# Thirteen modulation units added by GpSimd in place of VectorE, in a kernel of two transformer blocks

## The reference

```python
cs = jax.nn.silu(c)
mod = cs @ w_ada[l] + b_ada[l]
sh1, sc1, gt1, sh2, sc2, gt2 = [m[:, None, :] for m in jnp.split(mod, 6, axis=-1)]
h = _rmsnorm(x, g_pre_mix[l]) * (1.0 + sc1) + sh1
```

```python
h = rmsnorm(x, g_pre[i])
o, z = swa_sink_mixer(h, w_in_a[j], sinks_a[j])
y = (o.astype(z.dtype) * jax.nn.silu(z)) @ w_out
x = x + rmsnorm(y, g_post[i])
```

## Time and profile before

| | us |
|---|---|
| three runs | 1829.17, 1830.26, 1831.99 (median 1830.26) |
| the profiled execution | 1828.53 |
| its span in the trace | 1826.2 |
| TensorE busy in the span | 1798.2 (98%) |
| VectorE busy | 1294.4 (71%) |
| ScalarE busy | 895.6 (49%) |
| GpSimd busy | 189.0 (10%) |

### The profile page before, as it was taken

How to read it: one execution, slowest core, us unless ns; L and a number is a source line. 1 busy time by engine, 2 the same in 40 slices (tenths; PEclk the granted TensorE clock), 3 DMA queues, 4 the chain that set the end, 5 groups by cost and what they waited for, 6 DMA issues and landing times.

```text
span 1826.2 us, 25859 instructions
## 1 busy us (share of the span) xinstructions
PE 1798.2 (98%) x8412; PEld 1475.1 (81%) x8412; DVE 1294.4 (71%) x1700; ACT 895.6 (49%) x1265; POOL 189.0 (10%) x268
## 2 busy tenths in 40 slices
PE   8999999999999999999999999999999999999998
PEld 6777768887888888888888888888888888888886
DVE  5888888877977767777678887666666664455445
ACT  6566565455454454544444555444444444444443
POOL 1222221300000000110000130000000000000000
PEclk9999999999999999999999999999999999999999
DMA  8888768556667668698888957777777755555554
GB/s 282 277 270 261 259 215 323 182 171 189 223 217 251 211 215 272 210 321 282 285 281 284 319 186 230 230 230 230 230 230 230 229 191 191 194 195 193 192 191 138
DMA packets 180030, 424.91 MB, mean 233 GB/s; under 512 B 15376, under 2 KB 15616, under 8 KB 179584
## 3 DMA queue, kind: packets, MB, share of 16 engines
q1 hardware_dynamic: 151376, 320.07, 53.3%
q0 software_dynamic: 28304, 103.89, 18.1%
q10 hardware_dynamic: 288, 0.16, 0.1%
HBM read 421.97 MB, written 2.10 MB: 232 GB/s over the span
## 4 chain that ended last, share of the span: by engine, by line
PE 86%; DVE 6%; DMA 3%; ACT 2%; issue 2%; POOL 0%; DVEq 0%; ACTq 0%; POOLq 0%; SPq 0%
PE bank L1771 27%; PE bank L1773 27%; PE bank L1772 27%; DMA ada_raw<-in_w_ada 2%; PE bank L1827 2%; DVE w_lo L1119 2%; DVE acc_a L1129 1%; DMA raw<-in_w_in_a 1%; PE bank L1947 1%; DVE y L1261 1%; PE bank L1927 1%; ACT w_hi L644 1%; ACT y L653 0%; DVE x L1157 0%; PE bank L2066 0%
## 5 line engine op out<-in xcount | busy, mean ns | idle before, releaser
L1119 DVE TENSOR_TENSOR w_lo<-raw,w_hi 128x1024 fp32r<-128x1024 f32 (+1 forms) x608 | 742.4, 1226 | 412.6 <-ACT w_hi L644 411.8
L644 ACT ACTIVATE w_hi<-raw 128x1024 fp32r<-128x1024 f32 (+1 forms) x608 | 635.8, 1050 | 719.6 <-PE bank L1773 671.6
L1771 PE MATMUL bank<-w_hi,h_hi 128*128 128x512 f32 x2272 | 898.9, 396 | 4.3 <-DVE h_lo L1224 1.8
L1773 PE MATMUL bank<-w_hi,h_lo 128*128 128x512 f32 x2272 | 887.2, 391 | 0.0
L1772 PE MATMUL bank<-w_lo,h_hi 128*128 128x512 f32 x2272 | 886.0, 390 | 0.0
L1771 PEld LDWEIGHTS bank<-w_hi,h_hi 128*128 128x128 f32 x2272 | 427.6, 188 | 95.8 <-issue 3.9
L1773 PEld LDWEIGHTS bank<-w_hi,h_lo 128*128 128x128 f32 x2272 | 427.3, 188 | 91.2
L1772 PEld LDWEIGHTS bank<-w_lo,h_hi 128*128 128x128 f32 x2272 | 427.8, 188 | 85.3
L531 POOL DMA_DIRECT2D ada_raw<-in_w_ada x160 | 85.0, 531 | 1009.4 <-DVE acc_a L1129 812.6
L1129 DVE SCALAR_TENSOR_TENSOR acc_a<-ada_raw,cond,acc_a 128x1024 f32<-128x1024 f32 x112 | 143.1, 1278 | 16.1 <-DMA ada_raw<-in_w_ada 15.9
L1129 DVE SCALAR_TENSOR_TENSOR acc_b<-ada_raw,cond,acc_b 128x1024 f32<-128x1024 f32 x48 | 66.0, 1375 | 1.9 <-DMA ada_raw<-in_w_ada 1.9
(11 more groups left out here) (194 smaller groups left out, 1047.0 us busy)
## 6 DMA issues: line engine op xcount, KB each, us to landing
raw<-in_w_ff SPq DMA_DIRECT2D x256, 512.0 KB, 4.3
raw<-in_w_in SPq DMA_DIRECT2D x176, 512.0 KB, 4.5
ada_raw<-in_w_ada POOLq DMA_DIRECT2D x160, 512.0 KB, 5.0
raw<-in_w_in_a SPq DMA_DIRECT2D x72, 512.0 KB, 4.9
ada_more<-in_w_ada POOLq DMA_DIRECT2D x32, 512.0 KB, 5.9
raw<-in_w_out_a SPq DMA_DIRECT2D x32, 512.0 KB, 5.2
raw<-in_w_o SPq DMA_DIRECT2D x32, 512.0 KB, 4.9
raw<-in_w_moba SPq DMA_DIRECT2D x16, 512.0 KB, 4.5
```

The lines of the kernel that those rows point to most:

```text
L644: act.activation(used(w_hi, turn, s), used(raw, turn, s), ACT.Copy).then_inc(hi_ready, 1)
L1119: dve.tensor_tensor(used(w_lo, turn, s), used(raw, turn, s), used(w_hi, turn, s).bitcast(F32), ALU.subtract).then_inc(lo_ready, 1)
L1771: pe.matmul(out_ap, hi, rhs_hi, start=start, stop=False)
L1773: return pe.matmul(out_ap, lo, rhs_hi, start=False, stop=stop)
```

## The change

In each loop iteration GpSimd adds the units u2, u5 and u9 (of u0 to u11), and in the last iteration u0 to u3, all four. It does this with two instructions in place of VectorE's one: the loaded unit is multiplied in place by its number per partition, spread over 1024 columns, and a second instruction, which waits for the first through a new semaphore `ada_scaled`, adds it to the accumulator. `ada_done` becomes two semaphores, one for each half of the columns, because the units of the two halves may now finish out of order.

```diff
+ON_POOL, ON_POOL_LAST = (2, 5, 9), (0, 1, 2, 3)
...
-        ada_done = sem("ada_done")
+        ada_done = [sem("ada_done0"), sem("ada_done1")]
+        ada_scaled = sem("ada_scaled")
...
+            def add_group(i, n, nth):
+
+                part, k = group_k(i, n)
+                pool.wait_ge(ada_loaded[n % 4], (i * 12 + 8 + n - n % 4) * 4 + 16)
+
+                pool.wait_ge(ada_done[n % 2], i * 6 + 4 + n // 2)
+                half = (acc_b if part == SH1 else acc_a)[:, n % 2 * (D // 2):(n % 2 + 1) * (D // 2)]
+                pool.tensor_tensor(ada_slot(n % 4), ada_slot(n % 4),
+                                   cond[:, bass.ds(k + n // 2, 1)].to_broadcast([P, D // 2]), ALU.mult)                    .then_inc(ada_scaled, 1)
+                pool.wait_ge(ada_scaled, i * len(ON_POOL) + nth + 1)
+                pool.tensor_tensor(half, half, ada_slot(n % 4), ALU.add).then_inc(ada_done[n % 2], 1)
...
-            def ada_and_bias(i, units, steps):
+            def ada_and_bias(i, units, adds, steps):
...
                     for j in range(GROUP_A):
                         if steps[j] == n + 1:
                             bias(i, j)
+                    if n - 4 in adds:
+                        add_group(i, n - 4, adds.index(n - 4))
...
                     if s >= 4:
-                        ada_first(i * 12 + 8, s - 4, acc_b, i * 2 + (s - 4) // 2)
+                        if s - 4 not in ON_POOL:
+                            ada_first(i * 6 + 4, s - 4, acc_b, i * 2 + (s - 4) // 2)
...
-                if s >= 4:
-                    ada_first(44, s - 4, acc_b, 6 + (s - 4) // 2)
+                if s >= 4 and s - 4 not in ON_POOL_LAST:
+                    ada_first(22, s - 4, acc_b, 6 + (s - 4) // 2)
```

More of the change, by code:

```diff
@@ L524, in init_acc, with load_ada @@
                 pool.dma_start(acc[0:1, :], b_ada[:, part * D:(part + 1) * D]).then_inc(acc_init[n], 16)
-            def load_ada(m, slot, part, k, half, slots=2, first=False):
+            def load_ada(pairs, n, slot, part, k, slots=2, first=False):
+                half = n % 2
                 if not first:
-                    pool.wait_ge(ada_done, m - slots + 1)
+                    pool.wait_ge(ada_done[half], pairs + n // 2 - slots // 2 + 1)
                 col = part * D + half * (D // 2)
@@ L532, in load_ada, with load_tiles, load_first, group_k @@
                     .then_inc(ada_loaded[slot], 16)
-            def load_tiles(m, part, k, tiles=4):
+            def load_tiles(pairs, part, k, tiles=4):
                 for n in range(2 * tiles):
-                    load_ada(m + n, n % 2, part, k + n // 2, n % 2)
-            def load_first(m, n, part, k):
-                load_ada(m + n, n % 4, part, k + n // 2, n % 2, 4, isinstance(m, int) and m + n < 4)
-            def load_group(i, n):
[L545 to L548, removed]
+                    load_ada(pairs, n, n % 2, part, k + n // 2)
+            def load_first(pairs, n, part, k):
+                load_ada(pairs, n, n % 4, part, k + n // 2, 4, isinstance(pairs, int) and 2 * pairs + n < 4)
+            def group_k(i, n):
+                if n < 4 or n >= 12:
+                    return SH1, i * 2 + (2 - 6 if n >= 12 else 0)
+                return SC1, i * 4 + 2
+            def load_group(i, n):
+                part, k = group_k(i, n)
+                load_first(i * 6 + 4, n, part, k)
+            def add_group(i, n, nth):
+                part, k = group_k(i, n)
+                pool.wait_ge(ada_loaded[n % 4], (i * 12 + 8 + n - n % 4) * 4 + 16)
[5 more added lines that the diff above has]
+                pool.tensor_tensor(half, half, ada_slot(n % 4), ALU.add).then_inc(ada_done[n % 2], 1)
             def bias(i, j):
@@ L590, in _ @@
                 pool.wait_ge(heads_cur, i + 1)
-                ada_and_bias(i, range(12), STEPS)
+                ada_and_bias(i, range(12), ON_POOL, STEPS)
             pool.wait_ge(heads_cur, CHUNKS)
-            ada_and_bias(CHUNKS - 1, range(4 - ADA_AHEAD), STEPS_LAST)
+            ada_and_bias(CHUNKS - 1, range(4 - ADA_AHEAD), ON_POOL_LAST, STEPS_LAST)
             pool.wait_ge(h_lo_ready, H_NORM0 + UPT)
@@ L610, in _ @@
             with pool.Fori(0, 4) as g:
-                load_tiles(g * 8 + 64, GT1, g * 4)
+                load_tiles(g * 4 + 32, GT1, g * 4)
             for n in range(UPT):
-                load_ada(96 + n, n % 2, SH2, n // 2, n % 2)
+                load_ada(48, n, n % 2, SH2, n // 2)
                 if 1 <= n <= 4:
@@ L619, in _ @@
             with pool.Fori(0, CHUNKS - 1) as c:
-                load_tiles(c * 12 + 104, SC2, c * 2, 2)
-                load_tiles(c * 12 + 108, SH2, c * 4 + 4, 4)
-            load_tiles(140, SC2, 6, 10)
+                load_tiles(c * 6 + 52, SC2, c * 2, 2)
+                load_tiles(c * 6 + 54, SH2, c * 4 + 4, 4)
+            load_tiles(70, SC2, 6, 10)
             for j in range(8):
@@ L696, in round_sum @@
             def round_sum(n, part, units):
-                act.wait_ge(ada_done, units)
+                for half in range(2):
+                    act.wait_ge(ada_done[half], units // 2)
                 if n >= 2:
@@ L1120, in split, with add_ada, ada, ada_first @@
                                   ALU.subtract).then_inc(lo_ready, 1)
-            def add_ada(m, slot, acc, k, half, loads):
+            def add_ada(before, slot, acc, k, half, loads):
                 dve.wait_ge(ada_loaded[slot], loads)
-                if not isinstance(m, int) or m > 1:
-                    dve.wait_ge(ada_done, m - 1)
+                if not isinstance(before, int) or before:
+                    dve.wait_ge(ada_done[half], before)
                 part = acc[:, half * (D // 2):(half + 1) * (D // 2)]
                 dve.scalar_tensor_tensor(part, ada_slot(slot), cond[:, bass.ds(k, 1)], part, ALU.mult, ALU.add)\
-                    .then_inc(ada_done, 1)
-            def ada(m, n, acc, k):
-                add_ada(m + n, n % 2, acc, k, n % 2, (m + n - n % 2 - ADA_FIRST // 2) * 8 + 16)
-            def ada_first(m, n, acc, k):
-                add_ada(m + n, n % 4, acc, k, n % 2, (m + n - n % 4) * 4 + 16)
+                    .then_inc(ada_done[half], 1)
+            def ada(pairs, n, acc, k):
+                add_ada(pairs + n // 2, n % 2, acc, k, n % 2, (pairs + n // 2 - ADA_FIRST // 4) * 16 + 16)
+            def ada_first(pairs, n, acc, k):
+                add_ada(pairs + n // 2, n % 4, acc, k, n % 2, (pairs * 2 + n - n % 4) * 4 + 16)
             def y_stats(r, t, squares):
@@ L1410, in _ @@
                         gate_turned(i)
-                    ada_first(i * 12 + 12, s, acc_a, i * 4 + 4 + s // 2)
+                    if s + 4 not in ON_POOL:
+                        ada_first(i * 6 + 6, s, acc_a, i * 4 + 4 + s // 2)
             last = CHUNKS - 1
```

24 lines of the change are left out of this document (12 added, 12 removed).

## The result

| | before | after |
|---|---|---|
| runs on the same chip, median (lowest to highest), us | 1829.72 (1828.02 to 1831.99), 4 runs | 1846.91 (1845.96 to 1848.32), 4 runs |
| the profiled execution, us | 1828.53 | 1847.76 |
| its span, us | 1826.2 | 1846.1 |
| GpSimd busy, us | 189.0 | 260.5 |

The changed kernel is slower: 1.0093 times the time of before, 95% interval 1.0081 to 1.0104, or 17.2 us. The forecast was 1837.8 with a range of 1831 to 1845. The sign was right, the size was not: the time lies above the range.

A forecast was written before the change was run, and what follows sets the result against it. TensorE bounds the loops; only the last iteration, bound by a chain through VectorE, could win. 6.6 there plus 1.0 in the loops is 7.6 us on 1828.53: 1836.1, or 1837.8 as median of runs; range 1831 to 1845.

The forecast's parts named there:

- The prize: Last iteration: at most 3.7 us of TensorE waits and 1.8 of clock can be won, 5.5 in all.
- The price of the new instructions: On GpSimd a product takes 2.2 us and a sum 2.4, so a unit 4.6 (4.4 to 6.4).
- Holding up for whole instructions: VectorE's L1119, L1129, L1250 and L1343 can each be blocked for a whole GpSimd instruction, now 2.2 or 2.4 us.
- rival 1: VectorE keeps the turn where it asks first; h4 and h5 on time, 0.5 to 3.5 us slower, taken as same; chance 0.19.
- Rival 2: No holding up that matters: additions run beside VectorE, last iteration gains 4.4 us, 1825.9; chance 0.09.
- The last iteration: GpSimd and VectorE hold each other up in turn, heads come late, TensorE waits 6.6 us longer for h6.
- The cycle: Last iteration, from one head's neg_cur to the next: 7.3 us, against 5.3 before.
- h6 stays 6.6 late: Last iteration: behind u3 only b7 follows, so h6 keeps h5's lateness of 6.6 us.
- The sign for L1119: Last iteration: VectorE's L1119 (`w_lo`) rows would show above 3 us.
- The loop iterations: Holding mostly covered under a busy TensorE: 0.3 us for each iteration, 1 in all, from bounds of 0 and 1.5 each.
- rival 3: Forecast plus loop stalls of 1.5 to 2 us each, at h7 and h6: 1842 or so; chance 0.12.
- u9 falls into slots with no heads: Loop iterations: u9's product and sum meet no head's work; no price of its own was given.

The follow-up runs named there:

- e6: The kernel before with VectorE's four additions of the last iteration left out and done by nobody: 1824.34 us against 1829.27, -4.9.
- e5: Last iteration only, GpSimd writes zeros about as long in place of product and sum, four additions left out: 1825.72 us against 1829.27 before, -3.6.
- e9: Last-iteration-only kernel with each GpSimd product and sum cut into two instructions of 512 columns: 1832.16 us against 1829.48 before, +2.7.
- e2: GpSimd adds only u0 to u3 of the last iteration, loops as before: 1832.36 us against 1829.31 before, +3.05.
- e1: GpSimd adds u2, u5 and u9 in the three loop iterations, last iteration as before: 1843.92 us against 1829.31 before, +14.6.
- e4: GpSimd adds only u9 in the loops, nothing in the last iteration: 1832.61 us against 1829.31 before, +3.3.
- e8: GpSimd adds only u11 in each loop iteration, nothing else: 1838.51 us against 1829.27 before, +9.2.
- e11: GpSimd adds only u2 in each loop iteration, nothing else: 1828.56 us against 1829.48 before, -0.9.
- e12: GpSimd adds only u5 in each loop iteration, nothing else: 1837.40 us against 1829.48 before, +7.9.

## Why the prediction was right and wrong, point by point

**What bounds the kernel.** Right. The prize was put at 5.5 us at most, all in the last iteration, and is 4.9 (e6). A small slip: the chain behind 264.16 shows eight matmuls at the pitch of 0.43, not nine, so the clock's part was 1.6 us and not 1.8.

**The price of the new instructions.** A little high. Undisturbed, the product takes 1.89 to 1.91 us (2.2 taken, from the bias by length) and the sum 2.36 to 2.41 (2.4 taken, from `sum_lo`).

**Holding up for whole instructions.** Right, by e5 and e9, and it decides against rivals 1 and 2. Rival 2 asked for `neg_cur` at 0.23, rival 1 for h4 on time; `neg_cur` is at 1.65 to 1.69, and h4's is 4.5 us late. One argument against rival 1 was weaker than it read: ahead of the addition of 231.34 VectorE had a `w_lo` (230.20, 1.21 us) that ended at 231.41, so the addition could begin at most 0.06 us ahead of the bias of 231.47, and the pair doesn't tell who asked first.

**The last iteration.** The mechanism was right and the size too large: 6.6 forecast, 4.65 in the trace, 3.05 alone by e2's runs. Less the 15.0 us by which the iteration began later, the ends of `neg_cur` are late by 2.2 (h2), 3.4 (h3), 4.5 (h4), 5.7 (h5) and 4.5 (h6); forecast were 3, 2.6, 4.6, 6.6 and 6.6. Three terms failed. The cycle was put at 7.3 and is 6.5: between 275.98 and 280.65 the product takes 1.9 (2.2 forecast) and the sum, behind the rounding, 2.2 (2.4 forecast), and neg_cur's own 0.15 and the beginning of the bias lie beside other work. And "h6 stays 6.6 late" left something out: before, the interval from the end of h5's `neg_cur` to the start of h6's was 271.34 - 266.44 = 4.9 us with u3's addition in it. That addition is gone, and the interval is 290.85 - 287.13 = 3.7. I had counted each removed addition inside the stretched cycles, and forgot the last of them. The third goes the other way: h3's slot was to be shorter, 4.9 us (253.4 to 258.3), since the load of u3 lets VectorE in. It was 6.5 like the others, and h3 came 3.4 late and not 2.6. The sign for L1119 (above 3 us) also failed: `w_lo` stayed at 1.21, since the instruction that it meets is a bias, and that is the one that stands.

**The loop iterations.** This is the step that failed: 0.3 us each, from bounds of 0 and 1.5, and measured 4.0, 4.8 and 4.8 (14.6 in all in e1). Even rival 3, at 1.5 to 2 each, was too low. It failed at three points of the working.

First, u5 and h7. The text named "the product of u5 can start at 156.5, just ahead of its neg_cur". That pair does meet, one head earlier: product and h6's `neg_cur` are handed over 0.02 us apart. But the text asked only what the product holds, 2.2 less a cover of 1.9. The sum behind it then holds the addition that stands ahead of h7 for another 2 us, and by then the cover is used. The two waits are 0.96 and 1.15 in after, where forecast was 0.3.

Second, "u9 falls into slots with no heads". True, and no reason for a price of zero: those slots have the gate's chain, `l_cur` to `z_silu` to the turning. I had looked for what VectorE does for the heads, and not for every instruction of VectorE that TensorE waits for. e4 and e8 show the two halves of that chain.

Third, the covers were taken one at a time, each in full. In a chain they are one and the same: of TensorE's 6.5 us of waiting for `z_silu` in the loops, 3.7 come from u9 finding its cover already spent by u5.

The clock was a term for the last iteration alone, taken as 0. In the loops TensorE sets the time, and there a slower clock did cost: 1.5 us in each of two iterations of e1's trace, and nothing in after's.

u2, by contrast, was priced rightly at nothing (e11).

**The sum of the errors.** Loops 14.1 (17.2 less the 3.05 of e2) rather than 1.0, last iteration 3.05 rather than 6.6: 17.2 rather than 7.6, and the two errors even hid part of each other. The last line of the prediction had named its own failure: it is wrong "if the loop iterations stretch by more than the last".

## What to carry to other kernels

Work moved from VectorE to GpSimd can hold VectorE up for as long as each of its instructions runs, so it is priced by the chain that VectorE feeds at that moment, and a "free" engine's instruction of 2 us can make an instruction of 2 columns last 2 us. Before calling a stretch of a saturated kernel free, list every instruction there that the saturated engine waits for, with its cover, and spend each cover once along a chain. Where both engines are chained by semaphores, as the loads behind VectorE's additions here, their meetings come again in each iteration (within 0.1 us in e12), and must be placed, not averaged.

## What the runs showed of the hardware that I had not expected

- An instruction of VectorE with 16 columns and two inputs took 0.17 us alone and 2.08 beside a product of GpSimd. How small an instruction is doesn't protect it.
- The hold is not paid by one side alone. Of two instructions handed over 0.02 us apart, the product of 157.88 went first and `neg_cur` of 157.90 stood. In e12, at 96.48 and 96.57, `neg_cur` was first and took its 0.23, and the `w_lo` behind it stood. In the earlier trace rows, at 231.34 and 231.47, the one that was handed over first stood all the same, but the instruction ahead of it ended only at 231.41. The Trainium skill (SBUF — State Buffer, "Who interferes with whom") gives the turn to whoever issues first: the first two pairs agree, and the third can't tell, since a row's start is the hand-over and not the beginning of the work.
- Writes of GpSimd held `neg_cur` (up to 1.87 us) and let `w_lo` run.
- Behind TensorE's waits of 2.37 and 3.16 us in the last iteration, the granted clock over the stretch was 0.94, between its two levels of 1.2 and 2.4 GHz; at 269.16 four matmuls took 0.89 us that take 0.65 elsewhere. The same wait did not always lower the clock: behind 2.16 us in after it stayed at 1.00, behind 2.20 in e1 it fell to 0.97 over the next iteration.
